# Pairing expert blocks: one of up to 128 rows in three passes, one of up to 64 rows in two

## Chip, cores and metric

The kernel runs on one core of a Trainium2 chip. The metric is the device time in microseconds of one execution. In every time table below, "us" is measured from the start of the profiled execution's span.

## The reference, as far as it matters

Three transformer blocks run one after another over 512 tokens of width 1024. The change lies in the last part of the third: a mixture of experts with 32 experts, of which each token takes 4.

```python
def moe(h, router_w, router_b, w1, b1, w2, b2):
    logits = (h @ router_w + router_b).astype(jnp.float32)
    top_v, top_i = lax.top_k(logits, TOP_K)
    gates = jax.nn.softmax(top_v, axis=-1).astype(h.dtype)
    ...
    def expert_block(args):
        xb, e = args
        hid = xb @ w1[e] + b1[e]
        return clamped_swiglu(hid[:, :D_FF_3], hid[:, D_FF_3:]) @ w2[e] + b2[e]

    ys = lax.map(expert_block, (xs, blk_e)).reshape(-1, D)
    contrib = ys[dest] * gate_sorted[:, None]
    return jax.ops.segment_sum(contrib, tok_sorted, num_segments=T)
```

w1 of one expert is 1024 x 2048 and w2 1024 x 1024, so each expert has 12 MiB of float32 weights. On the reference's inputs the 2048 choices fall on the 32 experts so that each gets between 30 and 114 rows: 15 experts get more than 64 rows and 17 get at most 64.

## The kernel before

`route` ranks the chosen tokens within each expert, gives every expert as many blocks of 128 slots as its rows need, and writes tables: `row_of` (which token stands in which lane of a block), `gate_of`, `target_of` and `block_expert` (which expert a block belongs to, and in its last cell how many blocks are filled). It runs once, before the experts. VectorE does most of it in small operations of which each waits for the one before (`v.do`), with TensorE summing across partitions in between.

`experts` loops over the blocks in a hardware loop whose body holds two of them, s = 0 and 1, with buffers of their own for x, biases and gates. A block's work is the same for each:

- GpSimd gathers 128 rows of x with an indirect DMA (two blocks ahead), and scatters the block's result with an accumulating indirect DMA into `expert_sums`.
- SP loads the expert's weights in 12 halves of 1 MiB (`HALVES`): 8 up halves (unit u = h // 2, four units of 512 columns) and 4 down halves. The ring `experts_weights` holds 12 halves; SP may load a half again only when TensorE has consumed it (semaphore `consumed`).
- The products are float32 of almost full precision, made of two roundings: ScalarE casts a half to its leading bits (`mask`, into one of 4 buffers `leading`), VectorE subtracts to get the rest (`split_half`, in place in the ring), and TensorE makes three passes (`three_passes`): leading x leading (L506), leading x with rest weights (L507), rest x with leading weights (L508), each with 128 x 128 of x or hidden as the stationary operand and 512 columns of weights moving.
- Each unit opens with a matmul of `pick` and `bias` that puts the bias into PSUM. When it is consumed, VectorE clips its linear part (`clip`), ScalarE makes the silu (`open_unit`), VectorE multiplies them (`multiply_gate`), TensorE transposes the product (`turn_product`), ScalarE takes the hidden's leading bits (`mask_hidden`) and VectorE its rest (`split_hidden`). Then come the down halves 8 to 11, and ScalarE writes y times the gate (`keep_y`).
- TensorE transposes the next block's x (`turn_x`), ScalarE and VectorE keep its two parts (`keep_x`, `split_x`).

Each engine's order is written out by hand in `body`; semaphores count across blocks. At the start of the stage SP also stores zeros into `expert_sums` before it goes on to the fourth half of weights.

## Time and profile before

| What | Before |
|---|---|
| Median of three runs (lowest, highest) | 3590.0 us (3584.51, 3592.63) |
| The profiled execution's own time | 3588.77 us |
| Its span, mean granted TensorE clock | 3586.9 us, 0.933 |
| TensorE busy over the span | 3234.0 us (90%) |
| VectorE busy | 2305.6 us (64%) |
| ScalarE busy | 1503.8 us (42%) |
| HBM read and written | 610.12 MB and 30.46 MB |

The profile follows one execution. The time of a run is a little more than the span, which reaches from the first to the last instruction. Engines are named PE (TensorE), PEld (its weight loads), DVE (VectorE), ACT (ScalarE), POOL (GpSimd) and SP; a q behind a name is its sequencer. A line number is one of the kernel, and helpers such as L500 (the rest of a rounding) and L506 to L508 (the three passes) are shared by many callers, so tiles' names tell them apart. The expert loop is the last third of the span.

### The profile page before, as it was taken

To read this page: it belongs to the slowest core of one execution; us is meant where nothing else is said; L and a number is where in the kernel's file an instruction comes from. 1 tells how busy PE (TensorE), PEld (TensorE's weight loads), DVE (VectorE), ACT (ScalarE), POOL (GpSimd) and SP (SyncE) were. 2 spreads that over 40 slices of the span, in tenths; PEclk is the share of its full clock that TensorE was granted. 3 is DMA by queue.
4 is the path that set the end of the run, shared out by engine and by line. 5 is a ranking of instruction groups with operands and counts; after the bars stand their busy time and mean duration, and the time that the engine had idled before them with its cause. 6 is when DMAs were issued, how large, how long until landed. Compare 5 with 4: busy or idle time off the path is not lost. (4 is left out here: it accounts for less than half of the span.)

```text
span 3586.9 us, 48596 instructions
## 1 busy us (share of the span) xinstructions
PE 3234.0 (90%) x17450; PEld 2568.6 (72%) x17450; DVE 2305.6 (64%) x2968; ACT 1503.8 (42%) x1930; POOL 261.0 (7%) x194
## 2 busy tenths in 40 slices
PE   7888999999969978999878788879999999999996
PEld 5756787877857667788746565668888888888885
DVE  4375766343973454554545483468888888888885
ACT  1263222012232522200123153347777777777774
POOL 0000000000000000000000000012121212121221
PEclk8889999999989986999988899879999999999997
DMA  5411222232312000223273101179999999999994
GB/s 166 158 31 36 88 98 92 91 100 60 94 59 71 1 2 10 88 97 111 72 309 118 36 15 31 69 290 403 401 376 379 374 381 373 385 368 386 368 387 160
DMA packets 194350, 639.72 MB, mean 178 GB/s; under 512 B 13465, under 2 KB 113945, under 8 KB 139186
## 3 DMA queue, kind: packets, MB, share of 16 engines
q1 hardware_dynamic: 183954, 599.53, 44.5%
q0 software_dynamic: 9648, 35.13, 3.6%
q10 hardware_dynamic: 624, 3.35, 0.2%
q8 instruction: 84, 1.38, 0.2%
q14 instruction: 40, 0.33, 0.0%
HBM read 610.12 MB, written 30.46 MB: 179 GB/s over the span
## 5 line engine op out<-in xcount | busy, mean ns | idle before, releaser
L500 DVE TENSOR_TENSOR experts_rest<-experts_weights,experts_leading 128x2048 fp32r<-128x2048 f32 x386 | 879.1, 2285 | 49.6 <-ACT experts_leading L3174 46.8
L3174 ACT CAST experts_leading<-experts_weights 128x2048 fp32r<-128x2048 f32 x387 | 733.0, 1903 | 58.9 <-PE psum L508 25.8
L506 PE MATMUL psum<-experts_leading,experts_xT_leading 128*128 128x512 f32 x1024 | 403.1, 394 | 6.7 <-DVE experts_rest L500 6.7
L507 PE MATMUL psum<-experts_rest,experts_xT_leading 128*128 128x512 f32 x1024 | 405.0, 395 | 0.0
L508 PE MATMUL psum<-experts_leading,experts_xT_rest 128*128 128x512 f32 x1024 | 403.4, 394 | 0.0
L506 PEld LDWEIGHTS psum<-experts_leading,experts_xT_leading 128*128 128x128 f32 x1024 | 193.1, 189 | 51.6 <-DVE experts_rest L500 7.2
L507 PEld LDWEIGHTS psum<-experts_rest,experts_xT_leading 128*128 128x128 f32 x1024 | 193.3, 189 | 44.5
L508 PEld LDWEIGHTS psum<-experts_leading,experts_xT_rest 128*128 128x128 f32 x1024 | 193.2, 189 | 43.5
L506 PE MATMUL psum<-experts_leading,experts_hidden_leading 128*128 128x512 f32 x512 | 211.8, 414 | 0.3 <-DVE experts_hidden_rest L3261 0.3
L507 PE MATMUL psum<-experts_rest,experts_hidden_leading 128*128 128x512 f32 x512 | 201.4, 393 | 0.0
L508 PE MATMUL psum<-experts_leading,experts_hidden_rest 128*128 128x512 f32 x512 | 200.9, 392 | 0.0
L506 PE MATMUL psum<-ff_up_source_leading,ff_up_leading 128*128 128x512 f32 x352 | 139.2, 395 | 10.0 <-DVE ff_up_source_rest L500 10.0
L507 PE MATMUL psum<-ff_up_source_rest,ff_up_leading 128*128 128x512 f32 x352 | 139.4, 396 | 0.0
L508 PE MATMUL psum<-ff_up_source_leading,ff_up_rest 128*128 128x512 f32 x352 | 138.8, 394 | 0.0
L3083 POOL DMA_INDIRECT expert_sums<-experts_y,experts_targets x32 | 76.1, 2378 | 721.9 <-ACT experts_y L3196 721.9
L506 PEld LDWEIGHTS psum<-experts_leading,experts_hidden_leading 128*128 128x128 f32 x512 | 96.1, 188 | 29.8 <-DVE experts_rest L500 13.2
L3185 ACT ACTIVATE experts_silu<-psum 128x256 f32<-128x256 f32 x128 | 49.2, 385 | 159.0 <-DVE experts_lin L3248 158.9
L508 PEld LDWEIGHTS psum<-experts_leading,experts_hidden_rest 128*128 128x128 f32 x512 | 96.2, 188 | 22.2
L1566 ACT ACTIVATE merge_gate<-psum,parameters 128x512 f32<-128x512 f32 x32 | 22.1, 690 | 206.5 <-PE psum L508 206.5
L507 PEld LDWEIGHTS psum<-experts_rest,experts_hidden_leading 128*128 128x128 f32 x512 | 96.6, 189 | 16.3
L506 PE MATMUL psum<-erge_gate_source_leading,merge_leading 128*128 128x512 f32 x256 | 101.0, 395 | 6.7 <-DVE merge_gate_source_rest L500 4.7
L508 PE MATMUL psum<-erge_gate_source_leading,merge_rest 128*128 128x512 f32 x256 | 100.6, 393 | 0.0
(784 smaller groups left out, 6955.9 us busy)
## 6 DMA issues: line engine op xcount, KB each, us to landing
experts_weights<-in_w_up SPq DMA_DIRECT2D x259, 1024.0 KB, 9.5
experts_weights<-in_w_down SPq DMA_DIRECT2D x128, 1024.0 KB, 6.3
ada_unit<-in_w_ada SPq DMA_DIRECT2D x12, 2048.0 KB, 17.4
merge_first<-in_w_merge SPq DMA_DIRECT2D x16, 768.0 KB, 4.3
merge_weights<-in_w_merge SPq DMA_DIRECT2D x16, 768.0 KB, 4.3
ff_up_first<-in_w_up SPq DMA_DIRECT2D x11, 1024.0 KB, 4.8
ff_up_weights<-in_w_up SPq DMA_DIRECT2D x11, 1024.0 KB, 4.7
down_first<-in_w_down SPq DMA_DIRECT2D x8, 704.0 KB, 4.7
```

The source lines that it names most:

```text
L500: return dve.tensor_tensor(out, src, leading.bitcast(F32), ALU.subtract)
L506: pe.matmul(out, lh, rh, start=start, stop=False)
L507: pe.matmul(out, lh, rl, start=False, stop=False)
L508: return pe.matmul(out, ll, rh, start=False, stop=stop)
L1566: act.activation(gate[:, s, :], k.bank(2 * s), ACT.Sigmoid, bias=col(bias, n + q * N)).then_inc(opened[s], 1)
L3083: pool.indirect_dma_start(out=sums, out_offset=bass.IndirectOffsetOnAxis(ap=targets[:, s:s + 1], axis=0), in_=y[:, :, :].rearrange("p u n ...
L3174: act.copy(leading[h % LEADING], weights.half(h)).then_inc(masked, 1)
L3185: act.activation(silu[:, u % 2, :], unit_bank(u)[:, 0:HALF], ACT.Silu, scale=SWIGLU_ALPHA).then_inc(silued, 1)
```

## The change

The blocks are now paired. The body's first block (s = 0, `few`) holds up to 64 rows (`FEW`), the second (s = 1, `many`) up to 128. An expert's last block is small if it has at most 64 rows. If there are more small blocks than large ones, the surplus small ones stand in large places. On the inputs here that gives 16 pairs, and 32 blocks as before.

In `few` the stationary operand's 128 columns hold the leading part of x for 64 lanes and beside it the rest part for the same 64 lanes (`few_x`). Two passes, with the leading and with the rest weights, so give both parts' products, in PSUM's lower and upper 64 partitions. The two halves must be added: ScalarE copies the upper one to SBUF (`tail`, into the unused partitions of `bias`), and a matmul with `fold` adds it, and with it the bias, to the lower one (`fold_unit`). The same happens to y (`tail_y`, `fold_y`, `keep_few_y`), whose fold stands in the next block. The hidden of a few block holds its two parts side by side too. Gather and scatter of a few block move 64 rows. The new product also includes rest x rest, which the three passes leave out.

```diff
-            filled = eng.value_load(block_expert[0:1, SLOTS_MAX + 2:SLOTS_MAX + 3], min_val=1, max_val=SLOTS_MAX + 1)
-            with eng.Fori(0, (SLOTS_MAX + 1) // 2) as i:
+            filled = eng.value_load(block_expert[0:1, SLOTS:SLOTS + 1], min_val=2, max_val=SLOTS - 2)
+            with eng.Fori(0, SLOTS // 2 - 1) as i:
                 with eng.If(2 * i < filled):
                     body(i, 0, 2 * i)
-                    with eng.If(2 * i + 1 < filled):
-                        body(i, 1, 2 * i + 1)
+                    body(i, 1, 2 * i + 1)
...
+                def few(i, b):
...
+
+                        h = 2 * u + part
+                        high, low = weight_parts(h)
+                        pe.wait_ge(split, b * HALVES + h + 1)
...
+                        for n in range(KD // 2):
+                            kk = part * (KD // 2) + n
+                            pe.matmul(unit_bank(0, u), few_x[:, kk, :], high[:, n, :], start=kk == 0, stop=False)
+                            last = pe.matmul(unit_bank(0, u), few_x[:, kk, :], low[:, n, :], start=False, stop=kk == KD - 1)
+                        last.then_inc(consumed, 1)
+
+                    def fold_unit(u):
+
+                        pe.wait_ge(tailed, i * UNITS + u + 1)
+                        pe.matmul(unit_bank(0, u), fold[:, u, :], bias[:, 0, :], start=False, stop=True,
+                                  skip_group_check=True).then_inc(folded, 1)
...
+                    pe.wait_ge(x_split[0], i + 1)
+                    half(0, 0)
+                    half(0, 1)
+                    half(1, 0)
+                    pe.wait_ge(bias_landed[0], i * 16 + 16)
+                    fold_unit(0)
+                    half(1, 1)
+                    half(2, 0)
+                    fold_unit(1)
+                    half(2, 1)
+                    turn_product(0, 0, b * UNITS)
+                    half(3, 0)
+                    fold_unit(2)
+                    half(3, 1)
+                    turn_product(0, 1, b * UNITS + 1)
+                    pe.wait_ge(clipped, b * UNITS + 4)
+                    pe.wait_ge(silued, b * UNITS + 4)
+                    turn_x(1, i)
+                    fold_unit(3)
+                    pe.wait_ge(y_copied[0], b + 1)
+                    down(8, (0, 1)).then_inc(consumed, 1)
+                    turn_product(0, 2, b * UNITS + 2)
+                    pe.wait_ge(y_copied[1], b + 1)
+                    down(9, (0, 1)).then_inc(consumed, 1)
+                    turn_product(0, 3, b * UNITS + 3)
+                    down(10, (2,))
+                    down(11, (2,))
+                    down(10, (3,)).then_inc(consumed, 1)
+                    down(11, (3,)).then_inc(consumed, 1)
+
+                def many(i, b):
...
+                    def fold_y(u):
+
+                        pe.wait_ge(y_tailed, 2 * i + u + 1)
+                        pe.matmul(k.bank(2 + u), fold[FEW:P, 0, :], y_tail[FEW:P, u, :], start=False, stop=True,
+                                  skip_group_check=True).then_inc(y_folded, 1)
...
+                            passes(h, unit_bank(1, u), x_t, part * (KD // 2), KD // 2).then_inc(consumed, 1)
+                            if u == 0:
+                                fold_y(part)
...
+                    turn_product(1, 3, b * UNITS + 3)
                     down(10, (2,))
-                    turn_product(3, b * UNITS + 3)
                     down(11, (2,))
```

ScalarE and VectorE get an order of their own for each kind of block; these are their parts of few.

```diff
+                def few(i, b):
+                    def tail(u):
+
+                        act.wait_ge(consumed, b * HALVES + 2 * u + 2 + HALVES)
+                        if u:
+                            act.wait_ge(folded, i * UNITS + u)
+                        act.activation(bias[FEW:P, 0, :], unit_bank(0, u)[FEW:P, :], ACT.Copy).then_inc(tailed, 1)
+
+                    def tail_y(u):
...
+                        act.wait_ge(gates_kept[0], i + 1)
+                        act.activation(y_tail[FEW:P, u, :], k.bank(2 + u)[FEW:P, :], ACT.Copy).then_inc(y_tailed, 1)
+
...
+                    tail_y(0)
+                    act.wait_ge(bias_landed[1], i * 16 + 16)
+                    mask(2, b + 1)
+                    tail_y(1)
+
...
+                    def keep_few_y(u):
+
+                        act.wait_ge(y_folded, 2 * i + u + 1)
+                        act.activation(y[0:FEW, u, :], k.bank(2 + u)[0:FEW, :], ACT.Copy, scale=gate_slots[0:FEW, 0:1]).then_inc(y_copied[u], 1)
+
...
+                    unit = b * UNITS
+                    mask(3, b)
+                    mask(4, b)
+                    keep_few_y(0)
+                    keep_few_y(1)
+                    open_unit(1, 0, unit)
...
+                def clip(s, u, i, b):
+                    if s:
+                        dve.wait_ge(consumed, b * HALVES + 2 * u + 2 + HALVES)
+                    else:
+                        dve.wait_ge(folded, i * UNITS + u + 1)
...
+                    clip(0, 2, i, b)
+                    split_hidden(0, 0, b)
                     split_half(8, b)
-                    split_hidden(0)
-                    split_hidden(1)
-                    multiply_gate(2)
+                    multiply_gate(0, 2, b)
+                    clip(0, 3, i, b)
+                    split_hidden(0, 1, b)
                     split_half(9, b)
-                    clip(3)
+                    multiply_gate(0, 3, b)
                     split_half(10, b)
-                    multiply_gate(3)
-                    split_hidden(2)
+                    split_hidden(0, 2, b)
+                    split_x(1, i)
+                    split_hidden(0, 3, b)
                     split_half(11, b)
                     split_half(0, b + 1)
-                    split_hidden(3)
-                    split_x(1 - s, i + s)
+                    split_half(1, b + 1)
```

Routing ranks whole blocks, places large and small ones by separate sums, and has 64 slots instead of 48. Its changed core on VectorE:

```diff
-                v.do(dve.tensor_scalar(blocks[:, :], count_t[:, :], 0.0, None, ALU.is_gt))
+                v.then(dve.tensor_scalar(filled_by[:, :], count_t[:, :], 0.0, None, ALU.is_gt))
+                v.do(dve.tensor_scalar(large[:, :], count_t[:, :], float(FEW), None, ALU.is_gt))
                 for n in range(1, T // P):
-                    v.do(dve.scalar_tensor_tensor(blocks[:, :], count_t[:, :], float(n * P), blocks[:, :], ALU.is_gt, ALU.add))
+                    v.then(dve.scalar_tensor_tensor(filled_by[:, :], count_t[:, :], float(n * P), filled_by[:, :], ALU.is_gt, ALU.add))
+                    v.do(dve.scalar_tensor_tensor(large[:, :], count_t[:, :], float(n * P + FEW), large[:, :], ALU.is_gt, ALU.add))
+                v.do(dve.tensor_tensor(small[:, :], filled_by[:, :], large[:, :], ALU.subtract))
...
                 dve.wait_ge(started, 1)
-                dve.wait_ge(ranked, 1)
-                v.do(dve.tensor_scalar(start[:, :], k.bank(3, E), float(P), None, ALU.mult))
-                v.do(dve.tensor_tensor(slot[:, :, :], k.psum[:, 0:TT * E].rearrange("p (t e) -> p t e", e=E),
-                                       start[:, :].unsqueeze(1).broadcast_to([P, TT, E]), ALU.add))
+                v.do(dve.tensor_copy(starts[:, :], k.bank(3, 3 * E + 2)))
...
+                v.then(dve.tensor_tensor(large_of[:, :], large_upto, large_before, ALU.subtract))
+                v.then(dve.tensor_scalar(large_at[:, :], large_before, 2.0 * P, float(P), ALU.mult, ALU.add))
+                v.do(dve.scalar_tensor_tensor(width, smalls, larges, larges, ALU.max, ALU.add))
+                v.then(dve.tensor_scalar(last_odd, total_blocks, 2.0, -1.0, ALU.mult, ALU.add))
+                v.then(dve.tensor_scalar(last_even, total_blocks, 2.0, -2.0, ALU.mult, ALU.add))
+                v.then(dve.tensor_tensor(spread[:, :, :], whole_blocks[:, :, :], large_of[:, :].unsqueeze(1).broadcast_to([P, TT, E]),
+                                         ALU.is_ge))
+                v.do(dve.tensor_scalar(paired[:, :], small_before, 2.0, width, ALU.mult, ALU.is_lt))
+                v.then(dve.tensor_tensor(slot[:, :, :], slot[:, :, :], large_at[:, :].unsqueeze(1).broadcast_to([P, TT, E]), ALU.add))
+                v.do(dve.tensor_scalar(small_slot[:, :], small_before, 4.0, last_odd, ALU.mult, ALU.subtract))
+                v.do(dve.tensor_tensor(small_slot[:, :], small_slot[:, :], paired[:, :], ALU.mult))
+                v.do(dve.scalar_tensor_tensor(small_slot[:, :], small_before, -2.0, small_slot[:, :], ALU.mult, ALU.add))
+                v.then(dve.tensor_scalar(small_at[:, :], small_slot[:, :], last_even, float(P), ALU.add, ALU.mult))
+                v.do(dve.tensor_scalar(turned_slot[:, :], small_slot[:, :], last_odd, None, ALU.add))
```

Two places in the engines' rows show what moved. First VectorE near the end of a block, from the product of unit 3 on (ISA and REGISTER_ALU are waits' own instructions). Before:

```order
L3255 SCALAR_TENSOR_TENSOR experts_product<-experts_silu,experts_lin 128x256
L3261 SCALAR_TENSOR_TENSOR experts_hidden_rest<-psum,experts_hidden_leading 128x256
L3237 REGISTER_ALU
L500 TENSOR_TENSOR experts_rest<-experts_weights,experts_leading_16457 128x2048
L3237 ISA
L500 TENSOR_TENSOR experts_rest<-experts_weights,experts_leading_16456 128x2048
L3261 SCALAR_TENSOR_TENSOR experts_hidden_rest<-psum,experts_hidden_leading 128x256
L3241 REGISTER_ALU
L500 TENSOR_TENSOR experts_xT_rest<-psum,experts_xT_leading 128x1024
```

And in the new few block:

```order
L3454 SCALAR_TENSOR_TENSOR experts_product<-experts_silu,experts_lin 64x256
L3430 REGISTER_ALU
L500 TENSOR_TENSOR experts_rest<-experts_weights,experts_leading_16509 128x2048
L3462 SCALAR_TENSOR_TENSOR experts_hidden_leading<-psum,experts_hidden_leading 128x2x64
L3434 REGISTER_ALU
L500 TENSOR_TENSOR experts_xT_rest<-psum,experts_xT_leading 128x1024
L3462 SCALAR_TENSOR_TENSOR experts_hidden_leading<-psum,experts_hidden_leading 128x2x64
L3430 REGISTER_ALU
L500 TENSOR_TENSOR experts_rest<-experts_weights,experts_leading_16509 128x2048
```

One rest of weights (half 10) now stands behind the product of unit 3 and ahead of the hidden, and the rest of x and the last hidden stand ahead of half 11. Next TensorE between the last up half and the first down half of a few block:

```order
L3187 MATMUL psum<-experts_rest,experts_xT_few 128x512
L156 REGISTER_ALU
L3165 MATMUL psum<-constants,experts_product 128x64 x2
L3155 MATMUL psum<-constants,third_x_rows 128x128 x8
L3192 REGISTER_ALU
L3193 MATMUL psum<-experts_bias,experts_fold 128x512
L3228 REGISTER_ALU
L3200 REGISTER_ALU
L3205 MATMUL psum<-experts_leading_16508,experts_hidden_leading 128x512
```

Before, only the eight transposes of x stood there; now the turn of unit 1's product and the fold of unit 3 stand around them.

## Rows read from the trace of the kernel before

**Rows 1.** Busy time of each engine in two stretches of the expert loop.
```profile
core 0: us, PE busy (x) PEld busy (x) DVE busy (x) ACT busy (x) POOL busy (x), PEclk, DMA share, GB/s
...
2800.00:2900.00 100.00, 100.00 (x455) 80.84 (x454) 88.53 (x68) 74.42 (x64) 21.67 (x13) 1.00 0.99 373
2900.00:3000.00 100.00, 100.00 (x457) 80.90 (x456) 88.56 (x70) 75.29 (x65) 20.28 (x14) 1.00 0.98 382
```

**Rows 2.** Waits in the expert loop: total us, times, longest.
```profile
PEld psum L506 <- DVE experts_rest L500: 12.5, 31, 0.4
```

**Rows 3.** Waits of SP's queue, same stretch.
```profile
SPq L2971 <- PE psum L508: 814.1, 361, 4.1
```

**Rows 4.** Timeline of TensorE at a block's start and middle.
```profile
2850.19 0.39 PE L506 MATMUL psum<-experts_leading,experts_xT_leading 128*128 128x512 f32 x1
...
2850.42 0.39 PE L507 MATMUL psum<-experts_rest,experts_xT_leading 128*128 128x512 f32 x1
...
2867.28 0.60 PE L3111 MATMUL psum<-constants,experts_product 128*128 128x128 f32 x4
```

**Rows 5.** Timeline of VectorE in one block.
```profile
2855.93 0.42 DVE L3248 TENSOR_SCALAR experts_lin<-psum 128x256 f32<-128x256 f32 x1
2856.27 2.28 DVE L500 TENSOR_TENSOR experts_rest<-experts_weights,experts_leading 128x2048 fp32r<-128x2048 f32 x1
2858.47 0.42 DVE L3255 SCALAR_TENSOR_TENSOR experts_product<-experts_silu,experts_lin 128x256 f32<-128x256 f32 x1
...
2883.04 1.21 DVE L500 TENSOR_TENSOR experts_xT_rest<-psum,experts_xT_leading 128x1024 fp32r<-128x1024 f32 x1
2884.17 2.28 DVE L500 TENSOR_TENSOR experts_rest<-experts_weights,experts_leading 128x2048 fp32r<-128x2048 f32 x1
2887.45 4.67 DVE L500 TENSOR_TENSOR experts_rest<-experts_weights,experts_leading 128x2048 fp32r<-128x2048 f32 x2 [1.00 <-ACT experts_leading L3174]
```

**Rows 6.** Timeline of ScalarE in one block.
```profile
2851.73 3.71 ACT L3174 CAST experts_leading<-experts_weights 128x2048 fp32r<-128x2048 f32 x2
2856.47 0.38 ACT L3185 ACTIVATE experts_silu<-psum 128x256 f32<-128x256 f32 x1 [1.03 <-DVE experts_lin L3248]
2856.74 1.90 ACT L3174 CAST experts_leading<-experts_weights 128x2048 fp32r<-128x2048 f32 x1
...
2884.94 0.69 ACT L3196 ACTIVATE experts_y<-psum,experts_gate_slots 128x512 f32<-128x512 f32 x1 [0.84 <-PE psum L508]
```

**Rows 7.** Timeline of GpSimd: the first two scatters.
```profile
2418.36 2.40 POOL L3083 DMA_INDIRECT expert_sums<-experts_y,experts_targets  x1 [37.13 <-ACT experts_y L3196]
...
2454.53 2.40 POOL L3083 DMA_INDIRECT expert_sums<-experts_y,experts_targets  x1 [21.79 <-ACT experts_y L3196]
```

**Rows 8.** All engines from the routing stage to the first block.
```profile
2337.32 0.29 DVE L2903 TENSOR_TENSOR route_part<-route_hot,route_slots 128x128 f32<-128x128 f32 x1
...
2341.45 0.96 DVE L2915 TENSOR_TENSOR route_in_block<-route_edges 128x768 f32<-128x768 f32 x1
...
2345.91 0.19 DVE L2923 TENSOR_SCALAR third_block_expert<-psum 1x49 int32<-1x49 f32 x1
...
2368.18 0.77 PE L3128 MATMUL psum<-experts_bias,experts_pick 128*128 128x512 f32 x1 [4.79 <-DVE experts_xT_rest L500]
...
2376.53 2.88 SPq L2971 DMA_DIRECT2D experts_weights<-in_w_up  x5
```

**Rows 9.** Busy time, clock and DMA rate early in the expert loop.
```profile
2452.00:2488.00 36.00, 36.00 (x166) 29.11 (x165) 31.99 (x26) 26.87 (x24) 6.86 (x5) 1.00 1.02 407
```

**Rows 10.** DMA issues in a hundred us of the loop, with time to landing.
```profile
experts_weights<-in_w_up SPq DMA_DIRECT2D x21, 1024.0 KB, 9.0
```

**Rows 11.** Timeline of TensorE in the third block's attention.
```profile
2185.20 4.52 PE L912 MATMUL psum<-third_dk,third_mla_qn 128*128 128x512 f32 x8 [2.08 <-DVE mla_top L974]
```

**Rows 12.** Granted clock of two stretches before the expert loop.
```profile
2185.00:2190.00 5.00, 4.80 (x10) 2.38 (x12) 1.98 (x4) 1.25 (x4) 0.00 (x0) 0.66 0.00 0
...
1277.00:1282.00 5.00, 4.21 (x56) 3.03 (x52) 4.03 (x6) 0.00 (x0) 0.00 (x0) 0.50 0.00 0
```

326 lines of the change are left out of this document (221 added, 105 removed).

## The prediction

> **What bounds the kernel now.** I read the page's slices of the span first: in the last third, the expert loop, every digit repeats. The busy times of two stretches inside it [rows 1] are to be read next: TensorE is busy 100 us of 100 at the full granted clock, VectorE 88.6, ScalarE 75, and the DMA share is 0.98. Two resources look full, so the waits decide. TensorE hardly waits there: 12.5 us in 31 blocks [rows 2]. SP waits 814 us of the stretch for TensorE to consume a half of weights before it may load the next [rows 3]. So the transfers follow TensorE, and TensorE alone sets the pace. Its matmuls of 512 columns start 0.23 us apart [rows 4]. A block has 144 of them in three passes, 4 for the biases and 16 transposes (four took 0.60 us [rows 4]): 148 x 0.2295 + 16 x 0.14 = 36.2 us. The scatters of the first two blocks, 36.17 us apart [rows 7], agree. The engine has no slack inside a block.
>
> **What the change does to a block, TensorE first.** Of the 32 blocks, 17 have at most 64 rows and 15 more; a pair takes one of each, the odd small one stands in a large place, so 16 pairs run: 16 blocks in two passes ("few") and 16 in three ("many"), the same 32 loads of weights. Few has 96 matmuls, 4 folds in place of 4 bias matmuls, and 16 transposes of which half are narrower: about 25 us. Many keeps 36.17 and gets two fold_y (0.46) while half of its x transposes narrow (-0.2): 36.4. If nothing else limited, a pair would cost 61.4 against 72.3 us.
>
> **What limits a few block.** The weights still pass whole through ScalarE (cast) and VectorE (rest). From start to start a cast takes 1.81 us (3.71 for two, less 1.90 for the last) and a small activation 0.27 (2856.47 to 2856.74) [rows 6]; a rest takes 2.20 us, a small operation 0.34 and the rest of x 1.13 [rows 5]. VectorE in few: 12 x 2.20 + 8 x 0.34 + 4 x 0.2 (the hidden's split has half the columns, not shown by any row; between 0.1 and 0.34) + 1.13 = 31.1 us. ScalarE: 12 x 1.81 + 4 x 0.27 + six copies of 64 x 512, which no row shows; the nearest, 128 x 512, took 0.69 and is issued through in about 0.6 [rows 6] + hidden and x 1.8: 28.3 us. So VectorE, in program order, is the new bound of few, and what counts is how long it waits for fold chains.
>
> I laid the few block out from those durations, S = 0 being TensorE's first matmul. VectorE starts its third rest at 1.3, as it does now after a wait of 1.00 us [rows 5]. The first fold needs half 1 consumed (3.8) and ScalarE's tail copy, which stands behind a cast until 5.4: fold 6.15, clip 6.6, so VectorE waits 0.7. The next clips stand behind rests that end at 11.7 and 16.8, later than their folds, and wait for nothing. After the last up half (18.8) ScalarE copies the tail at 19.25, TensorE has meanwhile done the turns of x (8 x 0.14), folds at 20.1, and the fourth clip starts at 20.55 after a wait of 0.65. From there VectorE runs through: rest 9 to 23.3, product 3, rest 10 to 25.85, hidden, x, hidden, rest 11 to 29.6, rests 0 and 1 of the next block to 34.0. TensorE gets half 11 only at 29.6, after standing 2.6 us, and ends at 29.6 + 12 x 0.23 = 32.4. The many block then finds half 0 ready (31.8) and half 1 at 34.0, before it needs it (35.5), so it isn't delayed. **Few: 32.4 us, pair: 68.8 instead of 72.35.** Bounds: no better than VectorE's own 31.1, less what it can work ahead in the many block (at most the four leading buffers; some 2 us), so 29 to 30; no worse than if every one of the four folds held VectorE as the first does (0.7 each): 34.
>
> **The weights' transfers.** A half is 1.049 MB, so a pair moves 24 x 1.049 + gather and scatter of 192 rows of 4 KB, 1.57, + biases = 26.8 MB (now 27.3). Early in the loop, where the queue was behind and the share was 1.02, the chip moved 407 GB/s [rows 9]: 65.8 us a pair, 3 below 68.8. So the transfers do not bind, but hardly leave room; they land 9.0 us after issue now [rows 10], and have most of a block's time. The Trainium skill has a rule that speaks against this change: "DMA: Bandwidth & Descriptors", section Specifications, gives one core's share of HBM as about 358 GB/s. By it, an estimate, a pair would take 74.8 us and the change would lose 40 us over today's loop; the trace disagrees, with 407 GB/s measured here, so I don't follow it.
>
> **First block.** It takes 47.5 us now: TensorE begins at 2368.18 and the scatter of 2418.36 comes 2.7 us after its end [rows 7, 8]. SP issues the fourth to twelfth half only from 2376.5 [rows 8]; nine halves at 407 GB/s end at 2399.7, and cast, rest and the last down halves follow in about 7.5 us: 2407, that is 39 us and 8.5 saved.
>
> **Routing, on the path before the first block.** VectorE's chain of small dependent operations grows. Now a 128 x 128 operation steps every 0.32 us (0.29 in a row [rows 8]) and one of 32 columns about 0.2. Added ahead of the list of experts: before TensorE's sums four operations (+1.1), the number table 4 of 128 columns, of which 1.3 lies in the wait for the sums; after the sums 19 small ones in place of two, 4.2 more; one more turn through TensorE of about 0.9 on which VectorE waits. That is +5.8. Then edges, in_block and the block number widen from 48 to 64 slots: 0.96 for 768 elements [rows 8], so +0.27 each, +0.8. The nine small operations for fold stand ahead of the first x rest: +1.2, less 0.5 for a narrower x. Sum +7.5 to +8.2; I take 8.2 (bounds 5 and 11). Nothing hides it: the first load of weights waits for the list at 2345.91 and the first matmul for the placed rows [rows 8].
>
> **TensorE's clock.** The 2.6 us stand in each few block is a price by itself. In the third block's attention TensorE stood 2.08 us for VectorE before 2185.20 [rows 11], and the 5 us from 2185 show a granted clock of 0.66 [rows 12]: part of them at 1.2 GHz, costing 0.34 x 5 = 1.7 us of its work. The many block follows and has no slack, so a fall costs it that in full. There TensorE's work was thinner around the gap than here; I charge every second pair, 8 x 1.7 = 13.6 (bounds 0 and 27).
>
> **Sum.** Against the profiled execution's own 3588.8 us (span 3586.9; the median of the three runs is 3590.0, 1.2 above): 15 x (36.17 - 32.4) = -56.6; many 16 x 0.25 = +4; first block -8.5; routing +8.2; clock +13.6. Together -39: **3549 us**.
>
> **Rivals.**
> (1) *TensorE's clock stays.* If the stand makes no fall, 3536. A part of my own forecast's range.
> (2) *The clock falls for long; the one that ends on the other side.* After the gaps near 1270 the 5 us from 1277 stood at 0.50 [rows 12]. If each few block left 10 us at 1.2 GHz to the many block, a pair would lose 5 us: 3536 + 80 = 3616. It decides from 7.6 us at 1.2 GHz a pair: 3.8 us lost, 61 over 16 pairs, is 3597, slower by 0.2%. Against it: in many TensorE works without a gap, which in this trace brings 2.4 GHz back.
> (3) *The transfers bind.* If the rate under this pattern is today's 382 GB/s [rows 1] rather than 407, because a gather and a scatter of half as many rows disturb as much, a pair takes 70.1: 16 x 1.3 = 21 above 3536, 3557, and the clock's price comes in the shadow of it.
> (4) *VectorE works ahead.* If it enters few with two halves banked and the stand goes, the transfers' 65.8 is the pair: 3536 - 48 = 3488.
> (5) *More pairs than 16.* Would cost 36 us or more for each extra half pair; the reference's own choice of experts gives 15 and 17, so only if the placing went wrong. I leave it 0.01.
>
> **How the numbers follow.** Forecast with (1): 0.60. (3): 0.15. (4): 0.10. (2): 0.10 and a rest of 0.05 for costs I don't see, half of it above 3590. The range holds (1), (3), the few block's and the routing's bounds: 33 us for few at 34 instead of 32.4 and 3 more from the routing on the bad side, part of (4) on the good one: 3500 to 3585. Within 0.2%, 7 us, no change could be told. Faster 0.84, same 0.05, slower 0.11.
>
> **What would show it.** In the changed kernel's profile: scatters alternately about 32 and 36 us apart, or unevenly since few's stands inside many, but two of them 69 to 70; 32 scatters; TensorE's busy share near 0.96 in the loop and VectorE's above 0.93; TensorE's longest wait for the rests of half 11, some 2.5 us, 16 times; granted clock a little below 1.00 in the loop; DMA share 1.0 with 385 GB/s. The routing: first matmul of the loop near 2376. I am wrong if TensorE waits for transfers by way of ScalarE's casts, if the clips wait for folds by more than 1 us each, or if the clock in the loop is below 0.93.

## The result and the profile after

| | Before | Changed |
|---|---|---|
| First comparison: median (lowest, highest) | 3590.1 us (3583.3, 3594.1) | 3606.5 us (3597.4, 4802.1) |
| Ratio of the runs, 95% interval | | 1.0043 [1.0030, 1.0055] |
| Second comparison (`again`): median | 3593.8 us | 3602.0 us |
| Ratio, 95% interval | | 1.0020 [1.0010, 1.0030] |
| Span and mean granted clock of the profile shown | 3586.9 us, 0.933 | 3610.3 us, 0.921 |

The changed kernel is slower, by 0.2 to 0.4%. The prediction said 3549 us, range 3500 to 3585, and is wrong. The first profiled execution of the changed kernel took 4802 us in a disturbed run with a clock of 0.605, so every row "of the changed kernel" below is from a second one (`again`, 3612 us).

First its busy times in the stretches of [rows 1], then one short stretch of 3.4 us and one of 140 us, about two pairs of blocks:

```profile
core 0: us, PE busy (x) PEld busy (x) DVE busy (x) ACT busy (x) POOL busy (x), PEclk, DMA share, GB/s
2800.00:2900.00 100.00, 93.64 (x392) 71.25 (x393) 87.71 (x69) 76.02 (x70) 25.96 (x15) 0.97 1.00 382
2900.00:3000.00 100.00, 93.22 (x402) 70.27 (x400) 87.87 (x68) 79.77 (x73) 27.39 (x13) 0.98 0.98 362
...
2945.00:2948.40 3.40, 3.40 (x10) 2.65 (x9) 3.40 (x2) 0.82 (x2) 0.00 (x0) 0.55 1.00 417
2944.00:3084.00 140.00, 131.50 (x560) 99.20 (x560) 123.20 (x97) 110.73 (x102) 37.52 (x20) 0.98 0.99 372
```

TensorE went from 100 to 93 us of 100 (96 forecast), as it should with less work. VectorE did not rise: 88, and more than 93 was forecast. So the engine that was to be the new bound is not busier than before, and the mean clock is 0.97 where it was 1.00. The third row shows why: at the end of a few block, over 3.4 us, the granted clock is 0.55, so for most of them it is 1.2 GHz.

The scatters of GpSimd, the answer to [rows 7]:

```profile
2455.28 2.06 POOL L3135 DMA_INDIRECT expert_sums<-experts_y,experts_targets  x1 [46.49 <-ACT experts_y L3380]
...
2486.61 2.40 POOL L3135 DMA_INDIRECT expert_sums<-experts_y,experts_targets  x1 [21.55 <-ACT experts_y L3386]
...
2527.02 2.02 POOL L3135 DMA_INDIRECT expert_sums<-experts_y,experts_targets  x1 [25.87 <-ACT experts_y L3380]
...
2558.37 2.41 POOL L3135 DMA_INDIRECT expert_sums<-experts_y,experts_targets  x1 [21.55 <-ACT experts_y L3386]
```

Two scatters of few blocks are 71.74 us apart (2455.28 to 2527.02), against 2 x 36.17 before. A pair of blocks won 0.6 us where 2.7 were forecast (3.5 for the few block, less 0.85 for the clock). There are 32 scatters, so 16 pairs.

Now TensorE at the end of a few block. A row's first number is its start; the spacing of the starts is what to read:

```profile
3013.29 0.39 PE L3205 MATMUL psum<-experts_leading,experts_hidden_leading 128*128 128x512 f32 x1
3013.52 0.40 PE L3206 MATMUL psum<-experts_rest,experts_hidden_leading 128*128 128x512 f32 x1
3016.19 0.50 PE L3205 MATMUL psum<-experts_leading,experts_hidden_leading 128*128 128x512 f32 x1 [2.27 <-DVE experts_rest L500]
...
3017.80 0.63 PE L3206 MATMUL psum<-experts_rest,experts_hidden_leading 128*128 128x512 f32 x1
3018.23 0.63 PE L3205 MATMUL psum<-experts_leading,experts_hidden_leading 128*128 128x512 f32 x1
3018.66 0.63 PE L3206 MATMUL psum<-experts_rest,experts_hidden_leading 128*128 128x512 f32 x1
...
3020.64 0.40 PE L3258 MATMUL psum<-experts_bias,experts_pick 128*128 128x512 f32 x1
```

TensorE stands (is idle) 2.27 us for the rest of half 11, and 1 us after it resumes its matmuls come 0.43 us apart instead of 0.23, until shortly before the next block starts at 3020.64. This comes in each of the 16 pairs: the list of granted clocks has one fall at the end of every few block, 3.4 us long (6.8 us in the first), with 68.3 us at full speed between two. By the starts of the blocks a steady pair is a few block of 34.5 us and a many block of 37.2. The waits of the changed kernel from 2700 to 3490 (total, times, longest), against [rows 2]:

```profile
PEld psum L3205 <- DVE experts_rest L500: 45.4, 33, 2.7
PE psum L3205 <- DVE experts_rest L500: 33.1, 22, 2.3
DVE experts_rest L500 <- ACT experts_leading L3305: 30.8, 45, 1.7
...
PEld psum L3252 <- issue: 8.0, 22, 0.4
```

And VectorE in the same few block. It waits before the fourth clip and from there on does not pause; the rest of half 11 is the first of the three that begin at 3013.86, behind hidden, the rest of x (L500, 1.20) and hidden once more:

```profile
3007.06 0.41 DVE L3447 TENSOR_SCALAR experts_lin<-psum 64x256 f32<-64x256 f32 x1 [0.71 <-PE psum L3193]
...
3010.13 2.27 DVE L500 TENSOR_TENSOR experts_rest<-experts_weights,experts_leading 128x2048 fp32r<-128x2048 f32 x1
3012.33 0.27 DVE L3462 SCALAR_TENSOR_TENSOR experts_hidden_leading<-psum,experts_hidden_leading 128x128 fp32r<-128x128 f32 x1
3012.53 1.20 DVE L500 TENSOR_TENSOR experts_xT_rest<-psum,experts_xT_leading 128x1024 fp32r<-128x1024 f32 x1
3013.66 0.27 DVE L3462 SCALAR_TENSOR_TENSOR experts_hidden_leading<-psum,experts_hidden_leading 128x128 fp32r<-128x128 f32 x1
3013.86 6.67 DVE L500 TENSOR_TENSOR experts_rest<-experts_weights,experts_leading 128x2048 fp32r<-128x2048 f32 x3
```

The first few block is the other place, against [rows 8]. TensorE, ScalarE and SP in turn, all of the changed kernel:

```profile
2396.10 0.79 PE L3186 MATMUL psum<-experts_leading,experts_xT_few 128*128 128x512 f32 x1 [6.20 <-DVE experts_xT_few L500]
2414.64 0.80 PE L3193 MATMUL psum<-experts_bias,experts_fold 128*128 128x512 f32 x1 [11.31 <-ACT experts_bias L3338]
```

```profile
2409.58 1.90 ACT L3305 CAST experts_leading<-experts_weights 128x2048 fp32r<-128x2048 f32 x1 [13.53 <-DMA experts_weights<-in_w_up]
2412.07 1.90 ACT L3305 CAST experts_leading<-experts_weights 128x2048 fp32r<-128x2048 f32 x1 [0.59 <-DMA experts_weights<-in_w_up]
2413.99 0.59 ACT L3338 ACTIVATE experts_bias<-psum 64x512 fp32r<-64x512 f32 x1
```

```profile
2394.97 4.47 SPq L3106 DMA_DIRECT2D expert_sums<-experts_zero  x4
2404.30 2.87 SPq L3017 DMA_DIRECT2D experts_weights<-in_w_up  x5
```

SP asks for half 3 only at 2404.30, behind the zeroing of the sums. ScalarE waits for it 13.53 us, and the copy of the tail, which only the first fold needs, stands behind the casts of halves 3 and 4. So TensorE stands 11.31 us before the first fold.

For a budget with little of the scatter between executions, the time from the start of the experts' normalisation (moe_norm_sq, the last stage that the change leaves alone) is cut into parts, in us, each from its profile. What scatter is left shows in the first column, 37.4 and 39.5 for the same code:

| Kernel | to the lane numbers (route_lane_of) | to the first matmul | to the first scatter | to the last scatter | to the end | sum |
|---|---|---|---|---|---|---|
| before | 37.4 | 24.9 | 50.2 | 1121.4 | 47.1 | 1281.0 |
| control | 39.5 | 25.0 | 50.5 | 1121.2 | 46.4 | 1282.6 |
| changed (`again`) | 45.1 | 25.5 | 59.2 | 1107.4 | 47.5 | 1284.7 |
| `route_only` | 45.1 | 24.9 | 50.2 | 1122.7 | 47.9 | 1290.7 |
| `warm` | 45.1 | 25.5 | 56.5 | 1083.9 | 47.4 | 1258.4 |
| `rest11` | 45.1 | 25.5 | 56.9 | 1074.0 | 48.2 | 1249.7 |
| `ahead6` | 45.1 | 25.5 | 52.3 | 1107.6 | 48.1 | 1278.6 |
| `no_fold_y` | 45.1 | 25.6 | 58.0 | 1106.4 | 47.4 | 1282.5 |
| `y_order` | 45.1 | 25.5 | 59.3 | 1120.1 | 48.3 | 1298.3 |
| `before_ahead6` | 39.5 | 25.6 | 41.8 | 1121.5 | 47.1 | 1275.6 |
| `combined` | 45.0 | 25.5 | 50.0 | 1080.5 | 48.2 | 1249.2 |
| `rest11_no_fold_y` | 45.1 | 25.5 | 56.6 | 1054.5 | 48.0 | 1229.7 |
| `rest11_ahead8` | 45.1 | 25.5 | 42.9 | 1072.0 | 48.1 | 1233.6 |
| `rest11_ahead8_warm` | 45.1 | 25.6 | 43.0 | 1072.1 | 48.0 | 1233.8 |

A block's end is the first matmul of the next one. In the three-pass kernels a scatter comes 2.7 us after its block's end. In the others the few block's y is folded inside the next block, and its scatter comes 8.8 us after the end (first one of the changed kernel: block's end 2446.5, scatter 2455.28). So the third and fourth number columns compare directly among kernels of one kind only; between kinds, about 6 us move from the fourth to the third. The first block itself took 47.5 us before and 50.4 in the changed kernel.

### The profile page after: what moved, and what is told of

Its sections match the earlier page's. It is cut to its first block and busy times, and to the rows that moved or that the text cites. A ratio compares the mean times of both kernels' runs of the same rounds, so it can differ in the third digit from the quotient of the medians.

```text
span 4800.3 us, 47546 instructions
## 1 busy us (share of the span) xinstructions
PE 4442.1 (93%) x16724; PEld 2808.5 (59%) x16724; DVE 2303.8 (48%) x3003; ACT 1550.7 (32%) x2026; POOL 242.5 (5%) x195
## 5 line engine op out<-in xcount | busy, mean ns | idle before, releaser
L500 DVE TENSOR_TENSOR experts_rest<-experts_weights,experts_leading 128x2048 fp32r<-128x2048 f32 x386 | 877.9, 2281 | 87.7 <-ACT experts_leading L3305 86.4
L3186 PE MATMUL psum<-experts_leading,experts_xT_few 128*128 128x512 f32 x512 | 261.1, 510 | 10.8 <-DVE experts_xT_few L500 6.3
L3187 PE MATMUL psum<-experts_rest,experts_xT_few 128*128 128x512 f32 x512 | 260.9, 510 | 0.0
L506 PE MATMUL psum<-experts_leading,experts_xT_leading 128*128 128x512 f32 x512 | 260.1, 508 | 0.0
L507 PE MATMUL psum<-experts_rest,experts_xT_leading 128*128 128x512 f32 x512 | 259.6, 507 | 0.0
L508 PE MATMUL psum<-experts_leading,experts_xT_rest 128*128 128x512 f32 x512 | 259.2, 506 | 0.0
L508 PE MATMUL psum<-ff_up_source_leading,ff_up_rest 128*128 128x512 f32 x352 | 203.3, 578 | 0.0
L507 PE MATMUL psum<-ff_up_source_rest,ff_up_leading 128*128 128x512 f32 x352 | 202.6, 576 | 0.0
L3186 PEld LDWEIGHTS psum<-experts_leading,experts_xT_few 128*128 128x128 f32 x512 | 103.9, 203 | 77.2 <-issue 42.2
L3187 PEld LDWEIGHTS psum<-experts_rest,experts_xT_few 128*128 128x128 f32 x512 | 112.0, 219 | 55.2 <-issue 14.6
L507 PEld LDWEIGHTS psum<-experts_rest,experts_xT_leading 128*128 128x128 f32 x512 | 107.8, 210 | 56.9 <-issue 18.5
L506 PEld LDWEIGHTS psum<-experts_leading,experts_xT_leading 128*128 128x128 f32 x512 | 106.4, 208 | 59.1 <-issue 21.5
L508 PEld LDWEIGHTS psum<-experts_leading,experts_xT_rest 128*128 128x128 f32 x512 | 105.7, 206 | 58.8 <-issue 19.1
L508 PE MATMUL psum<-erge_gate_source_leading,merge_rest 128*128 128x512 f32 x256 | 130.6, 510 | 0.0
L507 PE MATMUL psum<-merge_gate_source_rest,merge_leading 128*128 128x512 f32 x256 | 130.3, 509 | 0.0
```

The lines of the kernel that those rows point to most:

```text
L500: return dve.tensor_tensor(out, src, leading.bitcast(F32), ALU.subtract)
L506: pe.matmul(out, lh, rh, start=start, stop=False)
L507: pe.matmul(out, lh, rl, start=False, stop=False)
L508: return pe.matmul(out, ll, rh, start=False, stop=stop)
L3186: pe.matmul(unit_bank(0, u), few_x[:, kk, :], high[:, n, :], start=kk == 0, stop=False)
L3187: last = pe.matmul(unit_bank(0, u), few_x[:, kk, :], low[:, n, :], start=False, stop=kk == KD - 1)
```

## The experiments

Times are medians; ratios are to the kernel before, with their 95% interval. All edits but three (`control`, `before_ahead6`, `route_only`) are to the changed kernel.

**The changed kernel once more, and the routing alone.** `route_only` has the new routing and place tables, and runs every block in three passes as before (its experts function is that of before, with 64 slots).

> The changed kernel once more, for a profile at the ordinary clock. Theory C (the clock falls in the stand at the end of every few block): the granted clock in the expert loop is 0.93 to 0.97, it falls once a pair, right behind TensorE's longest gap, and a pair takes 70 to 72 us. Theory T (few's chain is longer than laid out by hand): the clock stays at 1.00 in the loop and few takes 35 us or more, with clips that wait for folds by over 1 us. Theory D (transfers): casts wait for halves that have not landed, at a DMA share of 1.0. Time 3600 to 3610 in each.

> The new routing with its pairs and 64 slots, and every block still of 128 lanes in three passes as before. If routing costs what the prediction took: 8.2 us more than before (3598). If routing were the disputed part, 15 us or more. Also tells whether the order of the blocks matters for the loop: scatters still 36.17 us apart if not.

`again`: 3602.0 us, 1.0020 [1.0010, 1.0030]. Theory C holds: one fall a pair, behind the longest gap, a pair of 71.7 us, the clock in the loop 0.97 to 0.98. Theories T and D do not: a few block takes 34.5 us, the longest wait of a clip for a fold in the loop is 0.7 us, and no cast there waits for a landing.

`route_only`: 3606.3 us, 1.0031 [1.0019, 1.0043], 8 us above the 3598 expected. By the table the routing costs 5.6 to 7.7 us, and the loop and the end 2 to 3 more (blocks 36.22 us apart where they were 36.17, so the order of the blocks hardly matters). What is left of the 12.5 us stands in the stages ahead of the table. So the two-pass blocks, which should have won the routing back several times over, won 5.0 us from the first matmul to the last scatter (1171.6 to 1166.6): 8 in the loop, less the 3 that the first block lost.

**`control`**, the kernel before itself.

> The kernel before itself, unchanged, as a control. Ratio 1.000, within 0.001. In the profiles of the changed kernel the stages that the change does not touch already stood 5.6 and 19.7 us later than in the profile of the kernel before when the experts' normalisation began. If that is the scatter of one program from execution to execution, this second profile of the kernel before stands some 5 to 20 us off the first one at the same place; if it belongs to the changed program (another placement of its code or buffers), this profile stands within 2 us of the first one.

3593.2 us, 1.0006 [0.9995, 1.0016]. Its profile stands 2.8 us off the first at the normalisation, and the variant `before_ahead6` 3.3 us (2305.9, 2308.7, 2309.2). The eleven profiles with the changed routing stand at 2309.0 to 2325.5, mean 2314.7. So neither expectation holds cleanly: the scatter was large in the changed programs alone, of which there are more profiles, and their mean is 6.8 us later, over stages whose code is the same.

**`warm`**: fill the stand.

```
                     down(10, (2,))
+                    for _ in range(9):
+                        pe.matmul(k.bank(0), few_x[:, 0, :], weight_parts(10)[0][:, 0, :], start=True, stop=True)
                     down(11, (2,))
```

> The changed kernel with nine extra matmuls, whose result nobody reads, put into the stand of 2.27 us in which TensorE waits for the rest of half 11 in each few block. Theory one (the stand makes the clock fall, and the fall lies on the path): the granted clock stays at 1.00 from the first few block on, the twelve last matmuls of the few block come 0.23 us apart instead of 0.43, the few block is 1.7 us shorter and the pair of blocks 70.0 us instead of 71.7, so 16 pairs give about -27 us, a ratio of 0.9925 to the changed kernel (0.995 to the kernel before). Rival (VectorE, busy without a pause from the fourth clip on, sets the length of the pair, and the clock's fall lies beside it): the pair stays within 0.4 us of 71.7 and the time within 0.2% of the changed kernel's. A second rival (the clock falls for the engine's whole share of waits and not for this stand): the clock still falls once in each pair, somewhere else.

3577.5 us, 0.9966 [0.9953, 0.9979], faster than both kernels with more work in it. The stretch of 140 us, of `warm`:

```profile
2944.00:3084.00 140.00, 133.39 (x583) 100.63 (x582) 126.22 (x101) 112.99 (x104) 37.56 (x20) 1.00 0.99 382
```

The clock is 1.00 (0.98 in the changed kernel), and two scatters are 70.2 us apart (2928.03 to 2998.20 below) against 71.7. Theory one forecast 70.0. No few block's end has a fall any more, so the second rival is out. The block's other stands are all still there (1.05, 0.74, 0.46 and 0.43 us), so it is this stand that brings the fall, and the fall costs 1.5 us a pair.

```profile
2928.03 2.03 POOL L3135 DMA_INDIRECT expert_sums<-experts_y,experts_targets  x1 [24.27 <-ACT experts_y L3382]
...
2998.20 2.03 POOL L3135 DMA_INDIRECT expert_sums<-experts_y,experts_targets  x1 [24.29 <-ACT experts_y L3382]
```

**`rest11`**: take the stand away instead, by VectorE's order.

```
                     split_hidden(0, 2, b)
-                    split_x(1, i)
+                    split_half(11, b)
                     split_hidden(0, 3, b)
-                    split_half(11, b)
+                    split_x(1, i)
                     split_half(0, b + 1)
```

> The changed kernel with VectorE's order in the few block changed: the rest of half 11 ahead of the last piece of hidden and of the next block's x, which both come later instead. Theory one: TensorE's stand before half 11 shrinks from 2.27 to about 0.8 us (1.13 for x and 0.20 and the gap are moved behind it), the clock stays up, and the next block starts when the rest of half 0 is there, at 32.2 us after the block's start instead of 34.4: -2.2 us a pair, -35 us in all, a ratio of 0.992 to the kernel before. If the clock falls all the same: -0.5 us a pair. Rival (VectorE sets the pair by its sum of work, which this does not change): within 0.2% of the changed kernel.

3565.4 us, 0.9930 [0.9916, 0.9945]. Theory one, nearly to the number. TensorE's timeline of `rest11` at the same place:

```profile
2990.33 0.47 PE L3205 MATMUL psum<-experts_leading,experts_hidden_leading 128*128 128x512 f32 x1 [0.44 <-DVE experts_hidden_leading L3462]
2992.44 0.50 PE L3205 MATMUL psum<-experts_leading,experts_hidden_leading 128*128 128x512 f32 x1 [0.94 <-DVE experts_rest L500]
2995.32 0.40 PE L3258 MATMUL psum<-experts_bias,experts_pick 128*128 128x512 f32 x1
2995.97 0.50 PE L506 MATMUL psum<-experts_leading,experts_xT_leading 128*128 128x512 f32 x1 [0.26 <-DVE experts_rest L500]
```

The stand is 0.94 us, the twelve last matmuls take 2.88 (2992.44 to 2995.32) where they took 4.45, and the next block begins with a wait of 0.26 for the rest of half 0. The pair takes 69.4 us, and 70.4 twice; the list of clocks has 3 falls left, one of them at the end of the first block. VectorE's work is the same and the pair 2.3 us shorter, so the rival, that VectorE's sum of work sets the pair, is out.

**`ahead6` and `before_ahead6`**: six halves of the first weights asked for in the routing, in either kernel.

```
-AHEAD = 3
+AHEAD = 6
...
                 filled = blocks(pool, body)
+                for h in range(3, AHEAD):
+                    wait_apart(pool, landed[h], filled * 16 + 16, passed)
```

> The changed kernel with six halves of the first expert's weights instead of three asked for at the end of the routing (and six instead of three of a following expert at the end of the last block, 3 MB more). In the first few block TensorE stood 11.31 us before the first fold, since ScalarE's copy of the tail stands behind the casts of halves 3 and 4, which were asked for only behind the zeroing of the sums. Theory: that stand falls under 1 us, the first block goes from 50.6 to about 39.5 us, and the time by about -11 us (ratio to the kernel before 0.999). Rival (the transfers are bound by bandwidth there, so six halves delay the rows of x or the first halves, and what is won before the fold is lost before the first matmul): the first matmul comes 5 us or more later and the gain is under 4 us.

> The kernel before with six halves of the first weights asked for in the routing instead of three. Its first block takes 50.0 us from the first matmul to the first scatter where a later block takes 36.2, so a first block with its weights in time would give back up to 13.8 us. With the changed kernel the same edit gave 6.9 us in the first block by the profiles. Expected -7 us (ratio 0.998); if the transfers bind there (the halves 6 to 11 came late all the same), nothing.

`ahead6` 3595.5 us, 1.0012 [1.0000, 1.0025]; its first block is 6.9 us shorter (59.2 to 52.3), less than the 11 expected, and neither the time to the first matmul nor the loop moved. What was left, as TensorE's gaps in its first block: 3.76 us at 2393.56 and 1.80 at 2407.75, since halves 6 and 7 were asked for at 2389.49, behind the same zeroing:

```profile
2379.96 4.52 SPq L3106 DMA_DIRECT2D expert_sums<-experts_zero  x4
2389.49 0.97 SPq L3017 DMA_DIRECT2D experts_weights<-in_w_up  x2
```

`before_ahead6` 3585.9 us, 0.9981 [0.9971, 0.9992]; its first block went from 50.2 to 41.8 by the table, 47.5 to 39.0 by the starts of the blocks. The kernel before had the same flaw, so what `ahead6` repairs is for the most part not the change's doing.

**`no_fold_y`**: without the two matmuls that fold the few block's y.

```
-                            if u == 0:
-                                fold_y(part)
...
-                        act.wait_ge(y_folded, 2 * i + u + 1)
+                        act.wait_ge(y_tailed, 2 * i + u + 1)
```

> The changed kernel without the two matmuls that add the lower half of the few block's y onto its upper half in the next block (the product of the rest of hidden with the weights is missing from the sum). Theory: each such matmul has only 64 stationary rows, its weight load is not pulled ahead, and it takes 0.43 us and slows its neighbours, where the prediction had 0.23: a many block is 1.0 us shorter without the two, 16 of them -16 us to the changed kernel (ratio 0.998 to the kernel before). Rival (they cost 0.23 each, as predicted, and the rest is the clock): -0.46 us a block, -7 us.

3599.6 us, 1.0027 [1.0014, 1.0039], the same as with them. Its list of clocks has falls of 6.8 us instead of 3.4. By the starts of the blocks the many block became 0.9 us shorter (37.2 to 36.3), near theory's 1.0, and the few block, with the longer fall, 0.8 us longer (34.5 to 35.4): what the two matmuls gave, the clock took. The run's time alone says nothing about their price.

**`y_order`**: the casts ahead of the copies of y.

```
-                    keep_y(0)
                     act.wait_ge(bias_landed[0], i * 16 + 32)
                     mask(2, b + 1)
+                    keep_y(0)
                     keep_y(1)
...
                     split_half(3, b)
-                    clip(0, 0, i, b)
                     split_half(4, b)
+                    clip(0, 0, i, b)
```

> The changed kernel with ScalarE's cast of half 2 ahead of the two copies of y at the end of the many block, and VectorE's rest of half 4 ahead of the first clip in the few block. Theory: what is left of VectorE's waits in a few block (0.83 us before the rest of half 2 and 0.68 before the first clip) is one chain, from the copies of y over the casts to the tail and the first fold, and 0.7 us of it go: the pair is 0.7 us shorter, 16 of them -11 us. Rival (the chain has slack further on, at the fourth clip, which waits 0.71 for the fold): less than 0.2 us a pair.

3614.5 us, 1.0059 [1.0044, 1.0074]: a miss with the wrong sign, +12.7 us in the loop. The waits of `y_order`, same stretch as above:

```profile
ACT experts_silu L3322 <- DVE experts_lin L3447: 59.6, 55, 1.4
...
PEld psum L3193 <- ACT experts_bias L3338: 31.6, 33, 1.4
...
PE psum L3193 <- ACT experts_bias L3338: 19.4, 33, 1.0
```

ScalarE waits for a clip 55 times where the changed kernel has 44 in 11 pairs, one more in each few block, and TensorE waits for tails 19.4 us instead of 3.8. By the orders of the two engines, the first clip, moved behind a rest of 2.2 us, holds ScalarE's silu, and the second tail stands behind that silu. A pair took 72.3 us, 0.6 more than in the changed kernel. In four of the fifteen the fall of the clock was 6.8 us long as well, and they took 73.5, so some 5 of the 12.7 us are the clock's. I had followed the clip's own start and not who waits for it on the other engine.

**`combined`**: `rest11`, `ahead6` and `y_order` together.

> The changed kernel with the three edits together: VectorE's rest of half 11 ahead of hidden and x, six halves asked for in the routing, and the cast of half 2 ahead of the copies of y. If the gains add: -37 us (the first edit's measured gain to the changed kernel, ratios 0.993 and 1.003) -7 (the second's) -11 (the third's) = -55 us to the changed kernel, 3550 us or a ratio of 0.989 to the kernel before. If the transfers begin to bind (their share is 1.00 at 386 GB/s already with the first edit), the pair stays at 69.4 us and the time at 3560, a ratio of 0.991.

3563.3 us, 0.9935 [0.9916, 0.9955]. Neither expectation. Against `rest11` the table has -6.9 in the first block, as measured alone, and +6.5 in the loop for the order of y, half of its +12.7 alone. The pair is 69.9 us where `rest11` has 69.4: the same 0.6 us, and here no fall of the clock came with it after the first block.

**The last three**, at a steady or nearly steady clock: `rest11` without the two folds of y; `rest11` with eight halves ahead; and the latter with three extra matmuls in the stand that is left.

> The changed kernel with the rest of half 11 ahead, and without the two matmuls that fold y (the rest part of the few block's hidden is missing from y). Without that first edit the two matmuls came out as 0.1 us a pair, but the clock's fall had also grown from 3.4 to 6.8 us. Here the clock is steady. Theory: the two cost about 1.0 us, the pair goes from 69.4 to 68.4 us, 16 pairs -16 us. Rival (0.23 us each, as the prediction had it): the pair goes to 68.9 us. A third possibility: VectorE or ScalarE bind the many block after all, and nothing changes.

> The changed kernel with the rest of half 11 ahead and eight halves of the first weights asked for in the routing instead of three (and eight of a following expert at the end). With six, halves 6 to 11 were asked for only behind the zeroing of the sums and TensorE stood 3.76 and 1.80 us in the first block. Theory: those stands go, the first block to its first scatter goes from 52.3 to about 47 us, the pair stays at 69.4: about 3557 us, a ratio of 0.990 to the kernel before. Rival (the transfers of halves 6 and 7 delay those that are needed first, or the rows of x): the first matmul comes later and the total equals that with six, 0.992.

> As the run before, with three matmuls whose result nobody reads in the stand of 0.94 us that is left before half 11. The clock fell in 3 of 16 pairs with the rest of half 11 ahead and the pair took 70.4 us instead of 69.4 there. Theory: with the stand filled it does not fall, the pair is 69.4 throughout, -3 us against the run before (0.1%, at the limit of what the measurement tells). Rival: the three matmuls delay the last twelve by 0.2 to 0.7 us and the time grows by 3 to 10 us.

`rest11_no_fold_y` 3544.8 us, 0.9869 [0.9852, 0.9885]: 20.6 us under `rest11` by medians of two sets of runs, 19.5 in the loop by the table. Its pair is 68.1 us where that of `rest11` is 69.4 (two pairs with a fall of the clock took 69.7), so the two matmuls cost 1.3 us a pair, more than either number written down.

`rest11_ahead8` 3552.1 us, 0.9888 [0.9872, 0.9905]. The first scatter comes 42.9 us after the first matmul instead of 56.9, 4 us better than expected, and the clock stayed up:

```profile
2388.31 0.79 PE L3188 MATMUL psum<-experts_leading,experts_xT_few 128*128 128x512 f32 x1 [6.15 <-DVE experts_xT_few L500]
```

```profile
2431.20 2.06 POOL L3135 DMA_INDIRECT expert_sums<-experts_y,experts_targets  x1 [20.97 <-ACT experts_y L3382]
```

`rest11_ahead8_warm` 3553.9 us, 0.9899 [0.9882, 0.9915]. No fall of the clock in the loop in either, a pair of 69.4 in both: there was nothing left to warm, and the three matmuls hid in the stand.

`rest11_ahead8` is the best version that computes the whole result: 1.1% faster than the kernel before, and some 34 us faster than `before_ahead6`. That one has six halves ahead instead of eight, and its first block still takes 2.9 us more than a later one (39.0 and 36.2); a three-pass kernel with eight was not run.

## Why the prediction was wrong

The working was -39 us. From the normalisation on, the profile has +2.1 to +3.7 (1284.7 against 1281.0 and 1282.6); the medians differ by 8.2 us in the second comparison and 16.4 in the first, so the stages ahead of it would add about 5 and 13. Four terms failed, by 8 to 13 us each. In the loop none of the signs that the prediction named for being wrong appeared: no cast waits for a transfer, the clips wait for folds by 0.7 us at most, and the clock is 0.97 to 0.98. Only in the first block did TensorE wait for transfers by way of a cast. Point by point:

**What bounded the kernel before** was right: TensorE, with no slack.

**Routing, +8.2**: measured +7.7 and +5.6 against the two profiles of before, or +8.3 and +6.1 with the time to the first matmul. Right within its bounds, though its terms as written add up to 7.7 at most.

**The layout of the few block by hand** was right within half a us up to TensorE's stand. The fourth clip was forecast 20.55 us after the block's start and came at 20.96, the wait before it 0.65 and 0.71, VectorE's end 34.0 and 34.4, TensorE's stand 2.6 and 2.27 us. Without the fall of the clock (`warm`) the block takes 33.0 us where 32.4 was laid out.

**"I charge every second pair, 8 x 1.7 = 13.6" failed.** Of the twelve matmuls after the stand most ran at half clock, and the block ended at 34.5 instead of 32.4. I had the fall, but booked it for every second pair, from one row of another stage where TensorE's work around the gap was thinner. It comes every pair. `warm` prices it at 23.5 us over the loop; `rest11` gives 33.4, the fall and the 0.8 us a pair that the earlier half 11 wins besides. The term of 13.6 was 10 us too small. (In the first block the fall costs another 2.7 us, 59.2 less 56.5, which the budget counts under that block.) The rival "the clock falls for long" had the sign of the result, not its length: it wanted 7.6 us at 1.2 GHz a pair and there were 3.4. The result fell on that rival's side by the sum of the four terms.

**"Many keeps 36.17 and gets two fold_y (0.46)" failed.** A many block took 37.2 us (36.4 forecast). The rows of TensorE at such a fold:

```profile
2951.68 0.40 PE L508 MATMUL psum<-experts_leading,experts_xT_rest 128*128 128x512 f32 x1
2952.01 0.50 PE L3252 MATMUL psum<-experts_y_tail,experts_fold 64*128 64x512 f32 x1
2952.43 0.50 PE L506 MATMUL psum<-experts_leading,experts_xT_leading 128*128 128x512 f32 x1
2952.77 0.40 PE L507 MATMUL psum<-experts_rest,experts_xT_leading 128*128 128x512 f32 x1
```

From the matmul before the fold to the second one behind it is 1.09 us (2951.68 to 2952.77), where three steps of 0.23 make 0.69: the fold costs 0.63 in place of 0.23. The weight load's wait for "issue" in the waits of the changed kernel (22 times, 8.0 us, so 0.36 each) says that this load was not done beside the matmul before. The few block's transposes of the hidden, whose stationary operand has 64 rows too (L3165), show the same 0.36 us, 44 times; the loads of 128 rows between them (L507, L508) start with the matmul before. Two folds make 1.26, and `rest11_no_fold_y` measured 1.3. Over 16 pairs that is 20 us where the sum had 7.

**"First block 39 instead of 47.5" failed.** It took 50.4. The step took the arrival of nine halves at 407 GB/s for the limit. The transfers arrived in time once asked for; what counted was when SP asks for the fourth half (known from [rows 8], 8 us after the first matmul) and that ScalarE's tail for the first fold stands behind two casts of such halves. The order of operations laid out for a steady block was never applied to the first one. Forecast -8.5, measured +2.9: off by 11.4 us. In `rest11_ahead8` the first block took 33.8 us (2388.31 to 2422.11), better than the 39 forecast. The gain of the size forecast is there, but only once the weights are asked for earlier, and the three-pass kernel gains by that too (`before_ahead6`, 8.4 us).

**The transfers do not bind**: right. No cast waits for a landing in the middle of the loop, and the pair of 68.1 us in `rest11_no_fold_y` moves the same bytes. The Trainium skill, "DMA: Bandwidth & Descriptors", section Specifications, has about 358 GB/s as one core's limit, a stack's 716 GB/s divided by two cores. With one core at work that figure is passed here as in [rows 9]: the 3.4 us stretch above moved 417 GB/s, 140 us of `warm` 382.

**The sum.** From the first matmul to the last scatter -47.5 us was forecast (-8.5 - 56.6 + 4 + 13.6) and -5.0 measured. Of the 42.5 missing, 11 are the first block, 10 the clock and 13 the folds of y (20 less 7). The other 8 are 0.6 us in each of 15 few blocks (33.0 without the fall instead of 32.4): the fourth clip came 0.4 us later than laid out, and all behind it. No run was made on this last part. The range was too narrow as well: its 33 us for a few block of 34 are 16 x 1.6 = 26.

**What stays open**: why the stages ahead of the experts, unchanged in code, run later in the changed programs (mean 6.8 us, from 1 to 18 by execution). The placement of code or of buffers was not tried. If the medians hold the same lateness as the profiles, it makes up most of the 8.2 us between `again` and the kernel before, but less than half of the 16.4 us of the first comparison. Nor is it known why SP spends 4.9 us between the zeroing and the next request (2399.44 to 2404.30); its queue shows nothing there.

## What to carry to other kernels

When a change thins the work of the engine that had no slack, look at what follows each of its new stands: within 1 us of a stand of 2.3 us here came 3.4 us at half clock. Before giving such a change up, look for an operation ahead of the late one that nobody needs yet (here the rest of x, needed only at the next block's start): one line of order turned 0.2 to 0.4% slower into 0.7% faster. Lay the first turn of a loop out apart from a steady one, by the order of requests on every queue, and price an odd-shaped matmul with its neighbours, not by the step of the common shape.

## What was not expected of the hardware

The clock's fall repeats with great regularity: once in each of 16 pairs, 3.4 us long (6.8 in the first), after a stand of 2.27 us; filling the stand with nine matmuls that nobody reads removed all of them, while stands of up to 1.05 us stayed, and made the kernel 0.5 to 0.8% faster than without them. With a stand of 0.94 us a fall came 3 times in 16 pairs in each of two kernels (`rest11`, `rest11_no_fold_y`), and not once in `rest11_ahead8`, whose first block has no long stand. That the first block decides it was not shown: `combined`, whose first block stood too, has one fall at that block's end and none after it, and two of the falls of `rest11_no_fold_y` come deep in the loop, at 2973.8 and 3451.7 us. A matmul whose stationary operand has 64 rows cost 0.63 us among matmuls of 0.23.
